# Differential attention with one transposed difference of its two softmax maps, and head outputs evicted by ScalarE

## The reference

```python
s = jnp.einsum("bqhmd,bkhmd->bhmqk", qb, k).astype(f32) * scale
s = s - slopes[:, None, None, None] * dist
p = jax.nn.softmax(s, axis=-1)
a = p[:, :, 0] - lam * p[:, :, 1]
return jnp.einsum("bhqk,bkhe->bqhe", a.astype(v.dtype), v)
...
o = _rmsnorm(o, subln_g, SUBLN_EPS) * (1.0 - lambda_init)
return o.reshape(B, S, V_WIDTH) @ w_o
```

## Time and profile before

| what | value |
|---|---|
| median of 3 runs | 2388.68 us (2374.80 to 2389.15) |
| the profiled execution | 2385.95 us |
| its span, from first to last instruction | 2383.3 us |
| TensorE busy | 2248.0 us, 94% of the span |
| VectorE busy | 1543.7 us, 65% |
| ScalarE busy | 954.3 us, 40% |
| mean granted TensorE clock | 0.965 of full speed |
| loop of the differential attention, from the first scores to the output product | 2034.4 to 2146.9 us of the span |

### The profile page before, as it was taken

One profiled execution on the slowest core, in us unless ns is written; L12 is line 12 of the kernel. 1 busy time (PEld: TensorE's weight loads), 2 busy tenths in 40 slices (PEclk: granted clock), 3 DMA queues, 4 the chain that ended last, 5 costly groups with the idle time before them and its releaser, 6 DMA issues.

```text
span 2383.3 us, 42250 instructions
## 1 busy us (share of the span) xinstructions
PE 2248.0 (94%) x17761; PEld 2183.6 (92%) x17775; DVE 1543.7 (65%) x2069; ACT 954.3 (40%) x1208; POOL 103.0 (4%) x54
## 2 busy tenths in 40 slices
PE   7999869999999999999999998889999999979998
PEld 6999768999999998899999997779999998969998
DVE  6777764777777545665456558967557556576555
ACT  3334333433533444443344343134435334434433
POOL 0000000000000000000000003700000000000000
PEclk9999888999999987999999999999999999999999
DMA  7776431777576341045535542214454443322552
GB/s 317 300 282 262 173 118 66 297 298 285 229 283 265 142 176 54 1 171 216 178 141 188 182 161 104 89 71 162 177 191 154 182 178 122 142 89 102 193 181 88
DMA packets 52942, 417.61 MB, mean 175 GB/s; under 512 B 5872, under 2 KB 6000, under 8 KB 6768
## 3 DMA queue, kind: packets, MB, share of 16 engines
q1 hardware_dynamic: 52848, 416.27, 46.9%
HBM read 415.20 MB, written 1.05 MB: 175 GB/s over the span
## 4 chain that ended last, share of the span: by engine, by line
PE 79%; DVE 13%; ACT 3%; issue 2%; DMA 2%; POOL 1%; SPq 0%; DVEq 0%; ACTq 0%
PE AB L261 15%; PE AB L263 15%; PE AB L262 15%; PE Y L261 8%; PE Y L262 8%; PE Y L263 8%; DVE lo L1474 4%; DVE qT L2074 2%; ACT hi L1071 2%; PE Y L786 2%; PE M L576 2%; DMA raw<-slabs 1%; PE M L529 1%; PE N L819 1%; PE Y L801 1%
## 5 line engine op out<-in xcount | busy, mean ns | idle before, releaser
L1474 DVE TENSOR_TENSOR lo<-raw,hi 128x2048 fp32r<-128x2048 f32 x322 | 748.4, 2327 | 519.6 <-ACT hi L1071 519.3
L261 PE MATMUL AB<-h_hi,hi 128*128 128x256 f32 x3072 | 876.9, 285 | 11.9 <-DVE ada_raw L2084 5.8
L262 PE MATMUL AB<-h_lo,hi 128*128 128x256 f32 x3072 | 871.1, 284 | 0.0
L263 PE MATMUL AB<-h_hi,lo 128*128 128x256 f32 x3072 | 871.0, 284 | 0.0
L1071 ACT ACTIVATE hi<-raw 128x2048 fp32r<-128x2048 f32 x322 | 613.6, 1908 | 531.1 <-PE Y L263 285.5
L261 PEld LDWEIGHTS AB<-h_hi,hi 128*128 128x128 f32 x3072 | 591.6, 193 | 16.1 <-DVE ada_raw L2084 6.8
L262 PEld LDWEIGHTS AB<-h_lo,hi 128*128 128x128 f32 x3072 | 591.6, 193 | 0.1
L263 PEld LDWEIGHTS AB<-h_hi,lo 128*128 128x128 f32 x3072 | 591.4, 192 | 0.0
L261 PE MATMUL Y<-g_hi,hi 128*128 128x256 f32 x1280 | 362.2, 283 | 0.0
L262 PE MATMUL Y<-g_lo,hi 128*128 128x256 f32 x1280 | 362.2, 283 | 0.0
L263 PE MATMUL Y<-g_hi,lo 128*128 128x256 f32 x1280 | 362.2, 283 | 0.0
(11 more groups left out here) (309 smaller groups left out, 2348.5 us busy)
## 6 DMA issues: line engine op xcount, KB each, us to landing
raw<-slabs SPq DMA_DIRECT2D x322, 1024.0 KB, 4.8
ada_raw<-ada SPq DMA_DIRECT2D x35, 2048.0 KB, 7.8
kT<-ada SPq DMA_DIRECT2D x1, 1024.0 KB, 10.2
vt<-ada SPq DMA_DIRECT2D x1, 1024.0 KB, 12.2
x<-x_t SPq DMA_DIRECT2D x1, 1024.0 KB, 14.2
out_t<-x SPq DMA_DIRECT2D x4, 256.0 KB, 2.3
vec<-vectors SPq DMA_DIRECT2D x1, 462.0 KB, 3.7
hf<-constants SPq DMA_DIRECT2D x1, 401.0 KB, 14.4
```

The source lines that it names most:

```text
L261: nc.tensor.matmul(out_, w_hi, r_hi, start=start, stop=False, **kw)
L262: nc.tensor.matmul(out_, w_hi, r_lo, start=False, stop=False, **kw)
L263: return nc.tensor.matmul(out_, w_lo, r_hi, start=False, stop=stop, **kw)
L1474: nc.vector.tensor_tensor(lo[slot][:, :], raw[slot][:, :], hi[slot][:, :].bitcast(F32), ALU.subtract).then_inc(lo_done[slot], 1)
```

## The change

The output is linear in the map, so the difference can be taken ahead of the value product. With sums s1 and s2 of the two exponentials p1 and p2, the new kernel forms

p1 + (-lambda * s1 / s2) * p2

which is s1 times the wanted map. DVE does it in a new function `combine`: a reciprocal, a product of one column, and one pass over 128x256 in place. Only this one map is transposed (two tiles in the place of four), copied and multiplied with the values (two products in the place of four). The factor s1 isn't divided out of the output: the norm that follows would undo it, so the mean square is taken of the raw output and `s1 * s1 * 1e-5` is added in the place of 1e-5.

The raw outputs of a batch are moved out of PSUM by ACT (`evict`: a Copy of 128x256, and a Square of each head with its sum). What DVE has left of a batch is the norm, once for each pair.

```diff
+            def combine(G, gr):
+                s_ = diff_sums[:, gr["batch"] % 4, gr["sums"]:gr["sums"] + 2]
+                r = ratio[:, G % 2, :]
+                dve.wait_ge(p_ready, G + 1)
+                link(nc.vector.reciprocal(r[:, 0:1], s_[:, 1:2]))
+                link(nc.vector.tensor_scalar(r[:, 1:2], s_[:, 0:1], r[:, 0:1], small[:, 204:205], ALU.mult, ALU.mult))
+                p1, p2 = pr[:, G % 3, 0:T], pr[:, G % 3, T:2 * T]
+                nc.vector.scalar_tensor_tensor(p1, p2, r[:, 1:2], p1, ALU.mult, ALU.add).then_inc(maps_ready, 1)
...
 # DVE, attention(): behind the maxima of group s_
+                    if 1 <= s_ <= n and "maps" in groups[s_ - 1]:
+                        combine(g0 + s_ - 1, groups[s_ - 1])
...
 # PE, transposes()
-                    pe.wait_ge(p_ready, G + 1)
+                    if "maps" in gr:
+                        pe.wait_ge(maps_ready, g + 1)
+                    else:
+                        pe.wait_ge(p_ready, G + 1)
...
 # ACT, attention(): ahead of the exponentials of group s_, and behind the loop
+                    if evict and s_ >= lead + 2 and groups[s_ - lead - 1]["batch"] != groups[s_ - lead - 2]["batch"]:
+                        act.wait_ge(pv_done, G - lead - 1)
+                        evict(groups[s_ - lead - 2]["batch"], b0)
...
+                def evict(b_, b0):
+                    pair, t = divmod(b_, 2)
+                    if pair >= 2 and t == 0:
+                        act.wait_ge(ot_ready, pair - 1)
+                    at = pair * 2 * P
+                    o = out_bank(b0 + b_)[:, 0:2 * P]
+                    nc.scalar.activation(ot[:, t, at:at + 2 * P], o, ACT.Copy)
+                    for h in range(2):
+                        ins = nc.scalar.activation(hf[:, b_, h * P:(h + 1) * P], o[:, h * P:(h + 1) * P], ACT.Square,
+                                                   accum_out=head_sq[:, pair % 2, 2 * t + h:2 * t + h + 1])
+                    ins.then_inc(o_read, 1)
...
 # DVE, diff()
+                def batch(b_, bt):
+                    pair, t = divmod(b_, 2)
+                    if t == 0:
+                        return
+                    first = diff_sums[:, 2 * pair % 4:2 * pair % 4 + 2, 0:4:2]
+                    v4 = var[:, 0:4]
+                    link(nc.vector.scalar_tensor_tensor(v4.rearrange("p (t h) -> p t h", t=TT), first, 1e-5, first,
+                                                        ALU.mult, ALU.mult))
+                    link(nc.vector.scalar_tensor_tensor(v4, head_sq[:, pair % 2, :], 1.0 / P, v4, ALU.mult, ALU.add))
+                    rsqrt(rec[:, 0:4], v4, gf[:, 0:4])
                     o = ot[:, :, pair * 2 * P:(pair + 1) * 2 * P].rearrange("p t (h n) -> p t h n", h=2)
                     nc.vector.tensor_tensor(o, o, rec[:, 0:4].rearrange("p (t h) -> p t h", t=TT).unsqueeze(3
                                             ).to_broadcast([P, TT, 2, P]), ALU.mult).then_inc(ot_ready, 1)
-                def head_norms(pair):
-                    sq = hf[:, 0:2, :].rearrange("p t (h n) -> p t h n", h=2)
-                    o = ot[:, :, pair * 2 * P:(pair + 1) * 2 * P].rearrange("p t (h n) -> p t h n", h=2)
-                    link(nc.vector.tensor_tensor(sq, o, o, ALU.mult))
-                    link(nc.vector.tensor_reduce(rec[:, 0:4].rearrange("p (t h) -> p t h", t=TT), sq, AXX, ALU.add))
-                    link(nc.vector.tensor_scalar(var[:, 0:4], rec[:, 0:4], 1.0 / P, 1e-5, ALU.mult, ALU.add))
...
-                    reciprocals(bt, 4)
-                    link(nc.vector.tensor_scalar(rec[:, 1:4:2], rec[:, 1:4:2], small[:, 204:205], None, ALU.mult))
-                    g4 = gf[:, :].rearrange("p (h n) -> p h n", h=4)
-                    link(nc.vector.tensor_tensor(g4, out_bank(bt)[:, :].rearrange("p (h n) -> p h n", h=4),
-                                                 rec[:, 0:4].unsqueeze(2).to_broadcast([P, 4, P]), ALU.mult))
-                    nc.vector.tensor_tensor(ot[:, t, hp * 2 * P:(hp + 1) * 2 * P].rearrange("p (h n) -> p h n", h=2),
-                                            g4[:, 0:4:2, :], g4[:, 1:4:2, :], ALU.add).then_inc(o_read, 1)
```

More of the change, by code:

```diff
@@ L392, in diff_groups @@
                             nk=T, room=T, tiles=TT, batch=2 * pair + t, sums=(h % 2) * 2,
-                            keys=pair, values=pair,
-                            pv=[(((h % 2) * 2 + m) * P, [vt[:, j, h * P:(h + 1) * P] for j in range(TT)])
-                                for m in range(2)]))
+                            keys=pair, values=pair, maps=1,
+                            pv=[((h % 2) * P, [vt[:, j, h * P:(h + 1) * P] for j in range(TT)])]))
             return gs
@@ L797, in transposes @@
                     n = 0
-                    for u in range(len(gr["units"])):
+                    for u in range(gr.get("maps", len(gr["units"]))):
                         for t in range(gr["tiles"]):
@@ L1232, in operand, with attention @@
                 return c.take("hh", KD)
-            def attention(groups, lead, beside=None):
+            def attention(groups, lead, beside=None, evict=None):
                 g0 = c.take("grp", len(groups))
@@ L1241, in attention @@
                         act.wait_ge(t_ready, G - 2)
-                    if gr["sums"] == 0 and bt >= 3:
-                        act.wait_ge(o_read, bt - 2)
+                    if "maps" in gr:
+                        if gr["batch"] >= 4:
+                            act.wait_ge(ot_ready, gr["batch"] // 2 - 1)
+                        to_sums = diff_sums[:, gr["batch"] % 4, :]
+                    else:
+                        if gr["sums"] == 0 and bt >= 3:
+                            act.wait_ge(o_read, bt - 2)
+                        to_sums = sums[:, bt % 3, :]
                     for u in range(len(gr["units"])):
@@ L1251, in attention @@
                         beside[s_]()
+                for g in range(len(groups) - lead - 2, len(groups)):
+                    if evict and (g == len(groups) - 1 or groups[g + 1]["batch"] != groups[g]["batch"]):
+                        act.wait_ge(pv_done, g0 + g + 1)
+                        evict(groups[g]["batch"], b0)
             def turn(n_chunks, gain_=None, first=0):
@@ L1446, in diff @@
                 beside.update({12: lambda: turn_pair(0), 13: lambda: turn_pair(1)})
-                attention(diff_groups(), LEAD["diff"], beside)
+                attention(diff_groups(), LEAD["diff"], beside, evict)
                 turn_pair(2)
@@ L1859, in attention @@
                         if g == n - 1 or groups[g + 1]["batch"] != groups[g]["batch"]:
-                            dve.wait_ge(pv_done, g0 + g + 1)
                             bt = groups[g]["batch"]
+                            if "maps" in groups[g]:
+                                dve.wait_ge(o_read, b0 + bt + 1)
+                            else:
+                                dve.wait_ge(pv_done, g0 + g + 1)
                             batch(bt, b0 + bt)
```

16 lines of the change are left out of this document (7 added, 9 removed).

## The result

The changed kernel took 2368.95 us (median of 14 runs, 2363.94 to 2375.74). The kernel before took 2380.9 us beside it (14 runs, 2374.80 to 2389.15). The ratio is 0.995, with a 95% interval of 0.9938 to 0.9963: 12 us less, half a per cent (9 to 15 us by the interval). The profiled execution took 2368.51 us, with a span of 2366.6.

What follows compares the result with a forecast made beforehand. PE bounds the loop to step 11, then the uncovered chain PE, DVE, ACT, PE. 6.9 - 1.7 + 7.4 - 1.0 = 11.6 us less than the median 2388.68 gives 2377 us; forecast 2374 to 2381, wide range 2364 to 2388.

Steps and rivals of the forecast that it cites:

- PE work removed in the first part: Loop up to step 11: halved transposes and value products of the differential attention take 6.9 us off PE.
- The new waits: PE's transposes wait for `combine` on DVE 0.9 us each in steps 7 and 11, nowhere before: 1.7 us given back.
- Combine: DVE's reciprocal, one-column product and pass over 128x256 take 0.97 us in sum; bounds 0.85 and 1.3.
- Rival 2: `combine` at the critical place costs 1.6 us in all, at seven places: 4.4 us back, 2381 us; chance 10%.
- The eviction: ACT's Copy and two Squares per batch take 1.3 us, bounds 1.1 and 1.6; costs nothing up to step 11.
- The norm: DVE's norm of a pair falls from 4.36 us to 3.1, without its first three instructions.
- The second part: Scores of group 12 to the output product, without cover: 26.3 us where it was 33.6, 7.4 us less.
- The walk at full clock: Step-by-step timing from the scores of group 12, t = 0, reaching the output product at 26.3 us.
- The clock: Behind step 12, one more half-clock stretch like group 15's scores costs 1.0 us; the output product's extra 2.1 stays.
- Rival 1: PE's clock stays at 1.2 GHz from step 12 on: 2389 us, 3%; in part, 4.5 us, 2381 to 2384, 14%.
- rival 4: Shorter waits at the loop's end let the clock up earlier, 3 us more gain: 2373 us; chance 7%.
- No table load: ACT in the loop: no load added; were Square outside the exponential's set, two per batch would cost 20 us.

## Why the prediction came out right

The difference was predicted as 11.6 us and is 12. The time was predicted as 2377 us and is 2369. These two fit together because the three runs of before that were shown had a median of 2388.68, and the 14 runs beside the changed kernel one of 2380.9; 2380.9 - 11.6 is 2369.3. The narrow range of the forecast (2374 to 2381) missed for that reason, and the wide one held it because the runs' own spread had been put into it. The medians can't confirm the 11.6 closely, since their interval is 9 to 15 us; the stretches can, with 4.9 + 7.3 against 5.1 + 6.4. The steps, one by one:

- **PE work removed in the first part**, 6.9 predicted: 6.7, from the kernel without `combine`. Ten value products weigh 4.5 of it, as priced (4.45).
- **The new waits**, in steps 7 and 11 and nowhere before, 1.7 predicted: right in place and size. They show as 0.70 and 0.72 of idle time and cost 1.8 in all (73.59 - 71.79). Part of the gap may be that the idle time counts from the end of the last product, some 0.16 behind the moment in which the next could have started; that was not tested. Net 4.9, predicted 5.1.
- **Combine**, 0.97 predicted: 0.97 from its reciprocal's start to its end, its parts 0.15, 0.27 and 0.48. Rival 2 falls.
- **The eviction**, priced 1.3: 0.9. I had laid the three end to end; they overlap, and the second Square starts 0.25 behind the first. That is below my lower bound of 1.1. It is the one term mis-sized by more than its range, and only its last occurrence is in the chain: 0.4 us. PE's last wait is shorter by it too, 4.16 where 4.5 to 5 was forecast.
- **The norm**, 3.1 predicted: 3.05 (2125.88 to 2128.93).
- **The second part.** From the scores of group 12: scores of 13, 14 and 15 at 4.0, 8.9 and 12.5 (predicted 4.15, 9.1, 12.9), transposes of 14 and 15 at 17.3 and 19.5 (17.8, 19.7), the norm's end at 25.5 (25.8), the end of the last transposes at 26.7. The output product starts at 26.35. The walk at full clock said 26.3, and the same code at full clock throughout, with products in all waits, has 25.4: the walk was 0.9 too long, 0.4 of it the eviction and the rest small shares of the steps before (transposes of 15 at 19.2, predicted 19.7). With the clock it was 27.3 against 26.35, and so the term of the sum, 7.4 - 1.0 = 6.4, was 0.9 too small; 7.3 was measured.
- **The clock.** Two spells, as forecast, with 0.9 in the loop (predicted 1.0) and 2.0 in the output product (2.1, left as it was). The 1.0 was set as one more stretch like that of group 15; that it came out so exactly is luck, since the clock differs from execution to execution: with products at the end only, the same code up to there had one spell from step 13 on and reached the transposes of group 15 at 21.0, 1.8 later than at full clock (19.2). Rival 1 did not happen, in part either: it wanted 4.5 us in the loop. Nor did rival 4: the output product's first 21 products took twice their time before and after. The Trainium skill (TensorE: Matmul & The Clock Gate, section "What's actually happening") calls the throttled state the default, and the trace agrees in that the clock was 0.50 behind the waits of 3.58 and 4.16; the price was 3 us.
- **No table load.** No load stands in the loop; the next is at 2131.00, behind it. The rule that the prediction took from the Trainium skill (ScalarE: Activation LUTs, section "Table sets: the hidden batching unit") did not bite, since Copy and Square needed no other set than the exponentials have here. The 20 us of that case did not come.

The prediction added the parts as if each stood alone. They don't: without the eviction on ACT, 3 to 5 of the 12 us are left, because the gain of the smaller PE work then runs into longer waits.

## What to carry to other kernels

Before pricing work taken from the busiest engine, look at what the edit puts on the engine that it waits for: here halving PE's transposes and value products was worth 3 to 5 us by itself, and 12 only because three passes left DVE at the same time, at the places where PE waits behind a norm. Judge a small edit by a stretch between two named instructions rather than by the whole time: at the same clock the stretches repeat to some hundredths of a microsecond where medians move by several. Look at the granted clock in the stretch first, or what the clock did is put down to the edit. And an order that is right where there is cover (`combine` first) can be wrong where there is none, so set it for each part of a loop.

## What the runs showed of the hardware

Products that nobody reads, put into PE's last wait, went with a full clock in the output product: in the four kernels that had them its products followed each other by 0.12 us from the start, and in the others, with idle time there, by 0.21 at first. They are no help where the clock is low when they start. In one execution they began at a granted clock of 0.50 and took 4.03 us for twelve, against 3.18 for fourteen at full clock, and the work behind them came 1.5 us later than in the kernel without them.

The same instructions with the same waits don't always find the clock in the same state. In the kernel with products in step 15, PE behind the wait of 2.41 in step 13:

```profile
2116.42 0.44 PE L807 MATMUL Y<-ident,pr 128*128 128x128 f32 x2 [2.41 <-DVE pr L1883]
...
2117.22 1.06 PE L789 MATMUL Y<-ada_raw,qT 128*128 128x256 f32 x2
```

The scores take 1.06 in the place of 0.60; the changed kernel had the same wait of 2.41 there and went on at full clock to 2120.7. With the products at the end only the clock fell in step 13 as here, and with `combine` first one step later. Ahead of the loop, where the code is the same in all eleven kernels, the times differ too: the first scores of the loop started between 2027.2 and 2034.7 us in the eleven profiled executions. In the first 400 us the mean granted clock was 0.92 in the kernel before and 0.94 in the changed one:

```profile
0.00:400.00 400.00, 350.75 (x2727) 336.26 (x2727) 276.47 (x405) 150.75 (x187) 6.71 (x13) 0.94 0.58 226
```

That this makes up the scatter of the whole time is argued from these rows and wasn't tested.
